# The end of the FFN: last two down chunks interleaved, three half tiles kept in PSUM, seven gated on GpSimd

## What is computed

```python
h = _rmsnorm(x, p['g_pre_ffn']) * (1.0 + sc2) + sh2
f = (jax.nn.silu(h @ p['w_ffn_gate']) * (h @ p['w_ffn_up'])) @ p['w_ffn_down']
x = x + g2 * _rmsnorm(f, p['g_post_ffn'])
```

## Time and profile before

| | us |
|---|---|
| median of 3 runs | 1756.58 (1756.26 to 1757.56) |
| span of the profiled execution, first to last instruction | 1754.5 |
| TensorE busy / share of the span | 1697.7 / 97% |
| VectorE busy / share | 1049.5 / 60% |
| ScalarE busy / share | 641.5 / 37% |
| GpSimd busy / share | 87.2 / 5% |

### The profile page before, as it was taken

One profiled execution on the slowest core, in us unless ns is written; L12 is line 12 of the kernel. 1 busy time (PEld: TensorE's weight loads), 2 busy tenths in 40 slices (PEclk: granted clock), 3 DMA queues, 4 the chain that ended last, 5 costly groups with the idle time before them and its releaser, 6 DMA issues.

```text
span 1754.5 us, 30673 instructions
## 1 busy us (share of the span) xinstructions
PE 1697.7 (97%) x11952; PEld 1584.7 (90%) x11952; DVE 1049.5 (60%) x1929; ACT 641.5 (37%) x1327; POOL 87.2 (5%) x160
## 2 busy tenths in 40 slices
PE   5999999899999999999999999999999999999996
PEld 3778998799999998999998899999999999999995
DVE  2845458855665555343443434465667788888887
ACT  4433333332533332233333443332443343343342
POOL 0000000000222220000000000000010000000001
PEclk8999999999999999999999999999999999999998
DMA  9662333476524336754355856445332223233224
GB/s 358 212 253 88 122 98 104 124 226 205 183 93 144 114 130 207 243 169 148 112 182 178 255 202 213 166 144 174 89 123 58 73 74 96 81 89 97 73 81 148
DMA packets 238751, 259.89 MB, mean 148 GB/s; under 512 B 15143, under 2 KB 220647, under 8 KB 235536
## 3 DMA queue, kind: packets, MB, share of 16 engines
q1 hardware_dynamic: 210222, 228.88, 40.6%
...
...
## 4 chain that ended last, share of the span: by engine, by line
PE 76%; DVE 7%; issue 6%; PEld 4%; DMA 2%; DVEq 2%; ACT 1%; SPq 1%; POOL 0%; POOLq 0%; ACTq 0%; PEldq 0%
PE pj_acc L444 9%; PE pj_acc L446 9%; PE pj_acc L445 9%; PE pj_acc L451 5%; PE pj_acc L452 5%; PE pj_acc L453 5%; PE mx L2972 3%; PE mx L2974 3%; PE mx L2973 3%; PE pj_acc L2972 2%; PE pj_acc L2973 2%; PE pj_acc L2974 2%; PE mx L3038 2%; PE mx L3037 2%; PE mx L1858 2%
## 5 line engine op out<-in xcount | busy, mean ns | idle before, releaser
L444 PE MATMUL pj_acc<-pj_act_hi,pj_lo 128*128 128x320 f32 x1200 | 388.5, 324 | 8.3 <-DVE pj_act_lo L771 6.2
L446 PE MATMUL pj_acc<-pj_act_hi,pj_hi 128*128 128x320 f32 x1200 | 371.6, 310 | 0.0
L445 PE MATMUL pj_acc<-pj_act_lo,pj_hi 128*128 128x320 f32 x1200 | 371.3, 309 | 0.0
L451 PE MATMUL pj_acc<-pj_lo,pj_act_hi 128*128 128x256 f32 x880 | 254.5, 289 | 1.4 <-DVE pj_lo L371 0.7
L444 PEld LDWEIGHTS pj_acc<-pj_act_hi,pj_lo 128*128 128x128 f32 x1200 | 226.0, 188 | 32.7 <-issue 27.1
L452 PE MATMUL pj_acc<-pj_hi,pj_act_lo 128*128 128x256 f32 x880 | 248.9, 283 | 0.0
L453 PE MATMUL pj_acc<-pj_hi,pj_act_hi 128*128 128x256 f32 x880 | 248.8, 283 | 0.0
L445 PEld LDWEIGHTS pj_acc<-pj_act_lo,pj_hi 128*128 128x128 f32 x1200 | 226.4, 189 | 3.8 <-issue 3.4
L446 PEld LDWEIGHTS pj_acc<-pj_act_hi,pj_hi 128*128 128x128 f32 x1200 | 226.0, 188 | 0.0
L371 DVE TENSOR_TENSOR pj_lo<-pj_raw,pj_hi 128x1024 fp32r<-128x1024 f32 (+1 forms) x136 | 165.5, 1221 | 75.8 <-ACT pj_hi L362 72.1
L451 PEld LDWEIGHTS pj_acc<-pj_lo,pj_act_hi 128*128 128x128 f32 x880 | 168.4, 191 | 11.9 <-issue 10.4
...
## 6 DMA issues: line engine op xcount, KB each, us to landing
...
```

Of the source, the lines that this page charges most:

```text
L444: nc.tensor.matmul(out, lo[:, k, col], ahi[:, k, tok], start=(k == 0), stop=False)
L445: nc.tensor.matmul(out, hi[:, k, col], alo[:, k, tok], start=False, stop=False)
L446: last = nc.tensor.matmul(out, hi[:, k, col], ahi[:, k, tok], start=False, stop=(k == KT - 1))
L451: nc.tensor.matmul(out, ahi[:, k, tok], lo[:, k], start=(k == 0), stop=False)
```

## The change

Four things at the end. Down 9 and down 10 are no longer one behind the other: `LAST_ORDER` interleaves their units by token tile, and since `evicted` is false for down 9, its sum stays in the bank and down 10 adds to it there. Half tiles 7 to 9 take the place of 0 to 2 as the ones held in banks 5 to 7, are never copied out, and are squared (ScalarE) and gated (VectorE) straight from PSUM. Half tiles 0 to 6 are gated by GpSimd, each 128x512. `x1` and the gated rows get an area of their own (`ends`), so the x1 loads start one chunk earlier, and the steps ("last", t) stand behind units 11, 15, 17, 18 and 19 of the last twenty. Half tiles 7 to 9 are the first units of every down chunk now and 6 the last (`DOWN_ORDER`). The last unit thus reads columns of half c = 0 and the one before it of half 1, where it was the other way round; `held` follows (`9 - c_half`), and this changes the splits at the seams too.

```diff
-            b = WINO_BANK[x] if how == "wino" else u % 2 if how != "down" else 5 + x if x < 3 else (x - 3) % 4
+            b = WINO_BANK[x] if how == "wino" else u % 2 if how != "down" else Ffn.down_bank(self.chunks[n].dst, x)
             self.bank.append(b)
             self.rank.append(used[b])
-            used[b] += how != "down" or x >= Ffn.HELD
+            used[b] += how != "down" or Ffn.evicted(self.chunks[n].dst, x)
...
-                        held[b] = self.first[n] + (q if c.how == "wino" else 8 + c_half)
+                        held[b] = self.first[n] + (q if c.how == "wino" else 9 - c_half)
...
-    HELD = 3
-
-    def __init__(self, nc, m, norm, mod, g_post, y_rows, proj):
+    HELD = 7
+    DOWN_ORDER = (7, 8, 9, 0, 1, 2, 3, 4, 5, 6)
+    LAST_ORDER = [(0, x) for x in (7, 8, 9, 0, 1, 2, 3)] + [(1, 0), (1, 1), (0, 4), (0, 5), (1, 2), (1, 3), (1, 4), (1, 5),
+                                                           (0, 6), (1, 6), (1, 7), (1, 8), (1, 9)]
+
+    @staticmethod
+    def down_bank(i, x):
+        return 5 + x - Ffn.HELD if x >= Ffn.HELD else x % 4 if i < Ffn.NG // 2 - 2 else x % 5
+
+    @staticmethod
+    def evicted(i, x):
+        return x < Ffn.HELD and i != Ffn.NG // 2 - 2
...
+        rows = ends[:].rearrange("p a k t -> p a (k t)").rearrange("p a (t c) -> p a t c", t=NT)
+        self.x1, self.gated = rows[:, 0], rows[:, 1]
...
-            sp.wait_ge(self.proj.acc_full, self.proj.first[self.spare + 1] + 1)
+            sp.wait_ge(self.proj.acc_full, self.proj.first[self.spare])
             for t in range(NT):
-                sp.dma_start(self.x1[t], self.norm.x1_rows[t * P:(t + 1) * P, :]).then_inc(self.m.sem("x1_in%d" % t), 16)
+                sp.dma_start(self.x1[:, t], self.norm.x1_rows[t * P:(t + 1) * P, :]).then_inc(self.m.sem("x1_in%d" % t), 16)
...
+        opens = i == 0 or (x < self.HELD and i != self.NG // 2 - 1)
+        closes = i == self.NG // 2 - 1 or self.evicted(i, x)
...
-    def add(self, dve, u, nth, x, acc, read):
+    def add(self, dve, u, i, x, acc, read):
         E, nc = self.m.sem, self.nc
-        if nth == 0:
+        final = i == self.NG // 2 - 1
+        t, col = x // 2, slice((x % 2) * CB, (x % 2 + 1) * CB)
+        part = self.total[:, t, col]
+        if final and x >= self.HELD:
+            dve.wait_ge(E("squared"), x + 1)
+            nc.vector.tensor_tensor(self.gated[:, t, col], acc, self.gate_rows[:, 0 if t < NPT else 1, col], ALU.mult)
+            dve.drain()
+            return
+        if not self.evicted(i, x):
+            return
+        if i == 0 and x == 0:
             self.norm.x1_stored(dve, NT)
-        final = nth >= self.NG // 2 * 10 - 10
-        part = self.total[:, x // 2, (x % 2) * CB:(x % 2 + 1) * CB]
-        if x < self.HELD and not final:
-            return
         dve.wait_ge(self.proj.acc_full, u + 1)
-        if x < self.HELD:
-            nc.vector.tensor_copy(part, acc).then_inc(read, 1)
-        elif nth < 10:
+        if i == 0:
             nc.vector.tensor_copy(part, acc).then_inc(read, 1)
         else:
             nc.vector.tensor_tensor(part, part, acc, ALU.add).then_inc(read, 1)
-        if x == 9:
+        if x == self.DOWN_ORDER[-1]:
             dve.drain().then_inc(E("down"), 10)
         if final:
             dve.drain().then_inc(E("tile"), 1)
-            if x % 2 == 1:
-                self.gated(dve, x // 2)
...
+            col, x = slice(c * CB, (c + 1) * CB), 2 * t + c
+            if x < self.HELD:
+                act.wait_ge(E("tile"), x + 1)
+                own = self.total[:, t, col]
+            else:
+                u = self.proj.units.index((self.spare + 1, x))
+                act.wait_ge(self.proj.acc_full, u + 1)
+                own = self.proj.out(u)
...
+        for x in range(2 * t, min(2 * t + 2, self.HELD)):
+            col = slice((x % 2) * CB, (x % 2 + 1) * CB)
+            pool.wait_ge(E("tile"), x + 1)
+            nc.gpsimd.tensor_tensor(self.gated[:, t, col], self.total[:, t, col],
+                                    self.gate_rows[:, 0 if t < NPT else 1, col], ALU.mult).then_inc(E("gated"), 1)
...
+        dve.wait_ge(E("gated"), min(2 * t + 2, self.HELD))
         for c in range(2):
             col = slice(c * CB, (c + 1) * CB)
-            nc.vector.scalar_tensor_tensor(y[:, col], self.slot(t)[:, col], self.norm.stat[:, t, 2:3],
-                                           self.x1[t][:, col], ALU.mult, ALU.add).then_inc(E("y"), 1)
-
-    def slot(self, t):
-        return self.norm.junk[:] if t % 2 else self.gp[:]
-
-    def gated(self, dve, t):
-
-        if t >= 2:
-            dve.wait_ge(self.m.sem("y"), 2 * (t - 1))
-        self.nc.vector.tensor_tensor(self.slot(t), self.total[:, t], self.gate_rows[:, 0 if t < NPT else 1], ALU.mult)
-        dve.drain()
+            nc.vector.scalar_tensor_tensor(y[:, col], self.gated[:, t, col], self.norm.stat[:, t, 2:3],
+                                           self.x1[:, t, col], ALU.mult, ALU.add).then_inc(E("y"), 1)
...
-        v = u - len(proj.units) + 10
+        v = u - len(proj.units) + 20
         at = {"turned": u_up, "start": proj.first[ffn.spare] + 1, "rows": proj.first[ffn.spare] + 6,
               "x1": proj.first[ffn.spare + 1]}
-        plan += [(ffn, s) for s in ffn.STEPS if (v == min(2 * s[1] + 3, 9) if s[0] == "last" else u == at[s[0]] + ((3, 4, 6, 8, 9)[s[1]] if s[0] == "turned" else 0))]
+        plan += [(ffn, s) for s in ffn.STEPS if (v == (11, 15, 17, 18, 19)[s[1]] if s[0] == "last" else u == at[s[0]] + ((3, 4, 6, 8, 9)[s[1]] if s[0] == "turned" else 0))]
...
+        return [(len(chunks) - 1, x) for x in Ffn.DOWN_ORDER]
...
+    order += [(len(chunks) - 2 + last, x) for last, x in Ffn.LAST_ORDER]
```

More of the change, by code:

```diff
@@ L426, in multiply @@
         if c.how == "down":
-            return self.ffn.multiply(pe, self.nth[u], n, x, self.out(u), self.acc_full)
+            return self.ffn.multiply(pe, c.dst, n, x, self.out(u), self.acc_full)
         if c.how == "wino":
@@ L576, in dve_unit @@
             self.dve_last(dve, u - 2)
-            self.ffn.add(dve, u, self.nth[u], x, acc, read)
+            self.ffn.add(dve, u, c.dst, x, acc, read)
         if u and c.how not in ("wino", "down", "merge"):
@@ L3245, in layer @@
     with ExitStack() as own:
-        area(own, "no_").sb("yt", [P, 2, KT, T])
+        ends = area(own, "no_").sb("yt", [P, 2, KT, T])
         norm = Norm(nc, area(own, "no_", last), consts, mx, mod, a["g_post_mix"][0], x_rows, mod_cols, (act_hi, act_lo),
@@ L3249, in layer @@
     with ExitStack() as own:
-        ffn = Ffn(nc, area(own, "ff_", last, ("stored",)), norm, mod, a["g_post_ffn"][0], y_rows, proj)
+        ffn = Ffn(nc, area(own, "ff_", last, ("stored",)), norm, mod, a["g_post_ffn"][0], y_rows, proj, ends)
     with ExitStack() as own:
@@ L3435, in down @@
         chunks.append(Chunk("TM", "down", [(0, 2, rows)], i, units=10))
-        return [(len(chunks) - 1, x) for x in range(10)]
+        return [(len(chunks) - 1, x) for x in Ffn.DOWN_ORDER]
     up(0)
@@ L3445, in projection_chunks @@
             order += down(j // 2 - 1)
-    order += down(pairs // 2 - 2) + down(pairs // 2 - 1)
+    down(Ffn.NG // 2 - 2)
+    down(Ffn.NG // 2 - 1)
+    order += [(len(chunks) - 2 + last, x) for last, x in Ffn.LAST_ORDER]
     return chunks, order
```

18 lines of the change are left out of this document (6 added, 12 removed).

## The result

The changed kernel takes 1759.87 us (median; 1759.23 to 1761.46), the kernel before 1756.58 in the same comparison. The ratio is 1.0018, with an interval of 1.0012 to 1.0025: a small loss, and the interval leaves out 1. The span of the profiled execution is 1758.2 against 1754.5, so 3.7 us longer. One of the seven executions of experiment 2 ran at a granted clock of 0.66 and took 2382.68 us; it is left out of that experiment's median, and all others ran at 0.99.

What follows compares the result with a forecast made beforehand. The matmul engine was taken as the bound up to the end, VectorE in the last 20 us. Median 1756.58 + 4.0 (seams) - 2.6 (end) = 1758.0 us, range 1753.0 to 1761.5.

Steps and rivals of the forecast that it cites:

- both parts: Part 1, the end of the kernel, gains 2.6 us; part 2, the nine seams behind down chunks, loses 4.0 us.
- The lag at a seam: Behind down 8, q4's sum and low part stand behind the last add, so VectorE's L2942 comes 0.81 us late.
- rival (a): At the seams VectorE finds unseen slack that swallows the shift; 1754.0 us, down to 1751.2 with (b); chance 0.20.
- The slack of 0.51 and the 0.59: Ahead of x6: matmul follows VectorE's add start by 0.59 us when stalled, leaving 0.51 of slack before the change.
- The restart: First matmul step behind a stall is longer; 0.1 us more per seam, making a wait of 0.30 into 0.40.
- The number of stalls: One matmul stall at each of nine seams, 0.40 us each, plus 0.35 on the stall at 1696 behind down 8.
- the pause of 0.91: In a pair of wino chunks, a pause of 0.91 us was to take up what is left of the lag.
- The nine seams: Seams behind down chunks: 9 x 0.40 + 0.35 = 4.0 us lost; from below nothing, from above 5.8.
- The end: Last 20 us, bound by VectorE: gains 2.6 us with GpSimd gatings of 1.1; 2.9 with 1.04, 1.7 with 1.28.
- rival (b): At the end VectorE and GpSimd do not hold each other up; gain 5.4 us, total 1755.2; chance 0.08.
- Rival (c): At the end GpSimd becomes the bound, deciding from gatings of 1.65 on; total 1761.9 us; chance 0.17.
- Rival (d): Bank 4 or a bank of down 9 makes a matmul unit wait; small, within the range; chance: the rest.

Runs made afterwards that it cites:

- experiment 2: Kernel before with only the changed kernel's seams: last two units of down 0 to 8 change places, end untouched; 1761.98 us, ratio 1.0031.
- experiment 3: Changed kernel, but unit x6 of a wino chunk writes bank 1 instead of bank 3; 1760.05 us, ratio 1.0021.
- experiment 6: Changed kernel, but the ten combines at the end take their second tensor from a finished PSUM bank instead of x1; 1757.07 us, ratio 1.0005.
- experiment 1: Changed kernel with the seams put back to the old order of splits, the end staying as changed; 1754.46 us, ratio 0.9989.
- experiment 5: Changed kernel, GpSimd gating one column instead of 512 for half tiles 0 to 6, combines reading the ungated sum; 1756.84 us, ratio 1.0001.

## Why the prediction was right, and where its terms were off

The time (1758.0 forecast, 1759.87 measured) lies in the range, and the direction of both parts was right; the chance that it would come out the same within 0.2% was the largest, and the ratio of 1.0018 is there, near the edge to slower. What the prediction had wrong here is that a measurement tells apart only 0.2%, 3.5 us: the interval of 1.0012 to 1.0025 tells 3.3 us from nothing. Both terms came out on the slow side, so the sum is not right by errors that cancel. Point by point:

- **The lag at a seam** was forecast as 0.81 and is 0.88: L2960 starts 0.88 behind the start of the last add (0.20 of it idle, put down to "issue"), where I took 0.82. This alone makes the pause 0.37 instead of 0.30. That VectorE has no slack to take it back (rival (a) said that it has) held: it is busy 8.36 of the 8.96 us from 1680.84 to 1689.80.
- **The slack of 0.51 and the 0.59** from the start of an add to the matmul behind it held: 0.59 again for bank 3 (1688.64 to 1689.23), and 0.63 for bank 0 in experiment 3 (1651.38 to 1652.01).
- **The restart** was taken as 0.1 once for each seam. It is 0.08 twice, ahead of x6 and again at x0. I had held the second wait for a bank to be covered, and it is: bank 0's add starts at 1690.44, and x0 at 1691.07, one even step behind the matmul ahead of it. Why the step behind it is 0.22 no run shows.
- **The number of stalls.** I took one for each seam and 0.35 more behind down 8, and so it is: 0.83 there against 0.75, and in the pairs there is no second pause. It is not the pause of 0.91 that takes up the lag there, as I had it: it is 0.91 in the kernel after too (1656.46). In the pair behind down 7 VectorE makes up 0.23 us of the lag at its next wait for ScalarE, an idle 0.37 in the kernel before (first row) that is gone after (last row). The rest stays within the slack. The rows of before and after:

```profile
1654.08 1.23 DVE L405 TENSOR_TENSOR pj_lo<-pj_raw,pj_hi 128x1024 fp32r<-128x1024 f32 x1 [0.37 <-ACT pj_hi L398]
```

```profile
1656.46 1.22 DVE L405 TENSOR_TENSOR pj_lo<-pj_raw,pj_hi 128x1024 fp32r<-128x1024 f32 x1 [0.91 <-ACT pj_hi L398]
...
1659.03 1.23 DVE L405 TENSOR_TENSOR pj_lo<-pj_raw,pj_hi 128x1024 fp32r<-128x1024 f32 x1
```

- **The nine seams are not alike.** I read one seam closely and took it nine times. The one behind down 4 has 0.35 less of slack, by VectorE's idle 0.44 at 1523.70, which the trace of before showed. In all 4.0 was forecast and 5.3 to 5.5 measured, inside the upper bound of 5.8. This is the term that was mis-sized most: 0.12 in each of eight pairs (0.07 of lag, the rest restarts), 0.35 once and 0.08 behind down 8 make 1.4 by the traces.
- **The end** was forecast to gain 2.6 and gained 2.0 to 2.1. Laid over each other at the last matmul, my count and the trace agree to 0.15 until GpSimd's gating of half tile 3: add of 2 at 1727.9 (1733.60 - 5.79 = 1727.81), VectorE free behind tile 0's combines at 1731.0 (1731.1), adds until 1733.4 (1733.4). Then a gating takes 1.3 and not 1.1: the root of tile 1 is ready 0.36 late, tile 1's combines end 0.57 late, and 0.57 late is VectorE's end. My value from above, 1.28 by two operations of 256 columns, came within 0.02 of it, but that is luck, as those operations read one tensor and a broadcast column too. The estimate by the Trainium skill, "GPSIMD Engine Reference", section "Elementwise — side-by-side cycle accounting" (1.35), was nearer than the one row of the same size. That row had one tensor to read and the gating has two, which may be why it takes longer; no run tries it. What the prediction made of the longer gatings was too steep: it gave a gain of 1.7 with 1.28 and 1.3 with 1.35, and with 1.3 the gain is 2.06. In its own count four gatings lie on the path (of half tiles 2 to 5), which makes 2.6 - 4 x 0.18 = 1.9 with 1.28, and the combines held up by them take 0.69 each and not 0.77.
- **Hold-up of the engines** (rival (b) said there is none): forecast from the earlier trace rows, priced at 5.4 - 2.6 = 2.8, and 3.1 in experiment 6. The turns of tile 1 came as told: gating until 1741.51, combine until 1742.06, gating until 1743.21, combine until 1743.76, by the single instructions of the two rows. That the later one gets going about 0.14 ahead of the earlier one's end fits at tile 0 as well: 1734.41 + 1.30 - 0.14 = 1735.57, and two combines of 1.36 to the end of 1736.92.
- **Rival (c)** needed gatings of 1.65; they are 1.3. **Rival (d)**: no unit of down 9 or 10 waited for a bank. The gate rows came later than I had it (VectorE waited 1.67 for them until 1724.27 and was done 2.36 later, at 1720.8 by the clock of before, where I had 1720), and it cost nothing, as the next add was due at 1728.05.

That the loss at the seams comes from the splits and not from the new end is shown by experiments 1 and 2, that it is VectorE's lag through a bank by 3, and that the hold-up holds 3.1 us of the end by 5 and 6. What VectorE waits for in its idle 0.44 at 1523.70 the profile doesn't say, and no run tried it.
